# Attention scores scaled by their reciprocal sum on GpSimd in place of ScalarE, in a two-layer encoder on one core

## The chip, the cores and the metric

One Trainium2 chip, one of its cores. The metric is the device time of one execution in microseconds (us). The engines are called by the profile's names: PE is TensorE (PEld its weight loads), DVE is VectorE, ACT is ScalarE, POOL is GpSimd, SP is SyncE, which here issues the DMAs.

## What is computed

Two sequences of 512 tokens, width 1024, go through two layers with shared weights. Layer 0 mixes tokens by dilated window attention (12 heads of 64, in three groups with dilations 1, 4 and 16, ALiBi distances, RMS-normed queries and keys), layer 1 by a gated MLP over chunks; a gated MLP with a width-3 convolution follows each. All is float32. The attention part, cut to what matters here:

```
q = rmsnorm(q.reshape(B, S, N_HEADS_A, HEAD_DIM), g_q)
k = rmsnorm(k.reshape(B, S, N_HEADS_A, HEAD_DIM), g_k)
...
s = s - slopes[:, None, None] * dist
s = jnp.where(valid[:, None], s, NEG_INF)
lse = jax.nn.logsumexp(s, axis=-1)
p = jnp.exp(s - lse[..., None])
o = jnp.einsum('brnihm,brnmhd->brnihd', p, vw)
...
alpha = softmax(stack(lses, axis=0), axis=0)
o = concatenate([outs[g] * alpha[g][..., None] for g in range(N_GROUPS_A)], axis=2)
```

The softmax within a group times the softmax over the three groups is one softmax over the keys of all three groups. So the kernel puts the scores of three heads side by side, 768 columns in all, takes one maximum, one exponential and one sum over them, and multiplies the exponentials by one reciprocal.

## The kernel before

Every matrix product runs on PE; its inputs are split into a high and a low part (`..h` and `..l`, float32r) so that three cheaper products give float32 precision. The order of the work on each engine is written out by hand, and semaphores join the engines.

The change lies in the attention stage of layer 0. It has `NUNIT` = 32 units (2 sequences, 4 head triples `j`, 4 residues `rho`). A unit `n` is a tile of 128 queries by 768 keys (`KEYS`), and passes through these steps:

- PE `scores(n)` (L699 and L701): the three products of queries with keys, into banks 0 and 1.
- DVE `unit(n)`: L1578 adds the distances, in three pieces, into a buffer z; L1585 takes the maximum over its 768 columns and L1587 scales it to the bias of the exponential.
- ACT L1101: the exponential, in place in z, with the row sum in `smax[:, n % 3, 2:3]`.
- DVE `norm(n)` (L1562): the reciprocal of the sum, into `smax[:, n % 3, 3:4]`. It stands in `unit(n + 1)`, behind L1578 and ahead of L1585 there.
- ACT `normed(n)` (L1087): z times that reciprocal, in place. It raises the semaphore `z_done`.
- PE `turn(n)` (L712): waits for `z_done` and transposes the six 128-column blocks of z.
- ACT L1095 copies them from PSUM to `pT`; PE `values(n)` (L731 and L737) multiplies them with the values.
- After each fourth unit, ACT L1123 and L1124 copy the high parts of the outputs and DVE L1451 (`act1l<-bank,act1h`) subtracts them for the low parts.

There are three z buffers: `z[0]`, `z[1]` and the place of `rstd` (the rows write z for the first two and rstd for the third; units 0 and 1 use `z_first`). PE goes through iterations n: `scores(n)`, `turn(n - 2)`, `values(n - 3)`. ACT goes through: L1095 of unit n - 2, `normed(n - 1)`, the exponential of unit n, then what else is due.

The first units share the engines with the end of the step before, the norms of queries and keys: for each of 24 half tiles, ACT squares (L1059, or L1108 for the last two) and copies the high part (L1061, or L1110 for the last two), POOL subtracts it for the low part `sq_low` (L1998, a loop over all 24), PE sums both over the head's rows (L582 and L583), ACT takes the root (L1071) and DVE the reciprocal (L1527, or in halves at L1609). The last two half tiles come in ACT's iterations 0 and 2 of the units. On PE the sum of the last one stands ahead of `values(0)`. ACT needs another table for the root than for the exponential, so a table load stands at each change between them. POOL has nothing to do between its 24th subtraction and the squares of the step after attention.

Of the kernel before, what the change touches and what calls it, by code (L numbers as in the profile page):

```python
# [26 lines left out]
ACT = mybir.ActivationFunctionType  # L27
ALU = mybir.AluOpType
# [7 lines left out]
NS = 2  # L36
# [8 lines left out]
QK_TILES = 2 * KO  # L45
# [5 lines left out]
NUNIT = NS * 4 * R  # L51
# [58 lines left out]
def build(nc, xT, w_qkv, w_o, w_in, w_out, w_up, w_down, wsT, bs, vec, dist, squares, yT):  # L110
    with ExitStack() as ctx:
# [23 lines left out]
        smax, at = place("score_max", [P, 3, 4], F32, at)  # L135
# [52 lines left out]
        for layer, u_at, d_at in ((0, act2_at, act1_at), (1, act1_at, act2_at)):  # L188
            n = f"{layer}"
# [133 lines left out]
        z_rec = sem("z_rec")  # L323
        z_done = sem("z_done")
# [35 lines left out]
        def z_buf(n):  # L360
            if n < 2:
                return z_first[n][:]
            return z_sb[:, n % 3] if n % 3 < 2 else z2_sb
# [606 lines left out]
        def _(act):  # L970
            A = nc.scalar.activation
# [35 lines left out]
            for k, sl in V_ORDER:  # L1007
# [10 lines left out]
              scale=1.0 / D, bias=eps[:, 0:1]).then_inc(v_root, 1)  # L1018
# [61 lines left out]
            for r in range(2):  # L1080
                qk_step(QK_TILES * NS - 4, r, False, True)

            def normed(n):

                act.wait_ge(z_rec, n + 1)
                z = z_buf(n)
                A(z, z, ACT.Copy, scale=smax[:, n % 3, 3:4]).then_inc(z_done, 1)  # L1087

            for n in range(NUNIT + 3):
                u = n - 2  # L1090
                if 0 <= u < NUNIT:
                    act.wait_ge(t_mm, u + 1)
                    if u >= 2:
                        act.wait_ge(pv_mm, u - 1)
                    A(pT[:, u % 2], bank_flat[:, 2 * S:2 * S + KEYS], ACT.Copy).then_inc(t_ev, 1)  # L1095
                if 1 <= n <= NUNIT:
                    normed(n - 1)
                if n < NUNIT:
                    act.wait_ge(z_nmax, n + 1)
                    z = z_buf(n)  # L1100
                    A(z, z, ACT.Exp, scale=HD ** -0.5, bias=smax[:, n % 3, 1:2],  # L1101
                      accum_out=smax[:, n % 3, 2:3]).then_inc(z_exp, 1)
                if n in (0, 2, 4):
                    qk_sqrt(QK_TILES * NS - 3 + n // 2, n // 2 + 1)
                if n in (0, 2):
                    g = n // 2
                    act.wait_ge(up_ev, BANKS + UP_U - 1 + g)
                    A(sq[:], sumsq[:, g], ACT.Square).then_inc(qn_raw, 1)  # L1108
                    act.wait_ge(qn_raw, QK_TILES * NS - 1 + g)
                    A(sq_high[:], sq[:], ACT.Copy).then_inc(qn_high, 1)  # L1110
                if n in (8, 9):

                    if n == 8:
                        act.wait_ge(up_mm, UP_U)
                    ring_hi(WT_WO + n - 8, ows, owh)
                u = n - 3
                if u >= 0 and u % R == R - 1:

                    s, j = u // (4 * R), (u // R) % 4
                    pair = (u // R) % 2  # L1120
                    rows = slice(HD * (j % 2), HD * (j % 2) + HD)
                    act.wait_ge(pv_mm, u + 1)
                    A(act1h[:, j, s], bank[:, 4 + 2 * pair], ACT.Copy).then_inc(o_hi, 1)  # L1123
                    A(act1h[rows, 4 + j // 2, s], bank[rows, 5 + 2 * pair], ACT.Copy).then_inc(o_hi, 1)  # L1124
# [291 lines left out]
            for t in range(KD):  # L1416
                for s in range(NS):
                    n = u_group(t) + s
# [561 lines left out]
        def _(pool):  # L1980
            G = nc.gpsimd
# [11 lines left out]
                    for s in range(NS):  # L1993
                        add(m * NS + (n0 + s), 1, s, sq[:])

            with pool.Fori(0, QK_TILES * NS) as n:
                pool.wait_ge(qn_high, n + 1)
                G.tensor_tensor(sq_low[:], sq[:], sq_high[:].bitcast(F32), ALU.subtract).then_inc(qn_sq, 1)  # L1998
            def ffn(layer):
                mem = ffn_mem[layer]  # L2000
                w0, v0 = layer * NENT, layer * NWIN
# [112 lines left out]
```

## Time and profile before

| | us |
|---|---|
| median of 3 runs | 2043.03 (2042.94 to 2043.03) |
| the profiled execution, its own time | 2045.53 |
| its span, first to last instruction | 2043.7 |
| PE busy | 2008.1, 98% of the span |
| DVE busy | 1245.5, 61% |
| ACT busy | 943.2, 46% |
| POOL busy | 337.0, 16% |
| the attention units, first scores to last values | about 215 to 338 of the span |

All moments below count from the start of the span. The profile's busy shares are means over the whole span; the attention units take up only about 6% of it, so they have to be read on their own, from the timeline and from windows of the stretch. A bracket behind an instruction gives how long its engine sat idle before it, and which instruction ended that.

### The profile page before, as it was taken

To read this page: it belongs to the slowest core of one execution; us is meant where nothing else is said; L and a number is where in the kernel's file an instruction comes from. 1 tells how busy PE (TensorE), PEld (TensorE's weight loads), DVE (VectorE), ACT (ScalarE), POOL (GpSimd) and SP (SyncE) were. 2 spreads that over 40 slices of the span, in tenths; PEclk is the share of its full clock that TensorE was granted. 3 is DMA by queue.
4 is the path that set the end of the run, shared out by engine and by line. 5 is a ranking of instruction groups with operands and counts; after the bars stand their busy time and mean duration, and the time that the engine had idled before them with its cause. 6 is when DMAs were issued, how large, how long until landed. Compare 5 with 4: busy or idle time off the path is not lost.

```text
span 2043.7 us, 24674 instructions
## 1 busy us (share of the span) xinstructions
PE 2008.1 (98%) x9316; PEld 1657.5 (81%) x9316; DVE 1245.5 (61%) x1687; ACT 943.2 (46%) x1445; POOL 337.0 (16%) x238
## 2 busy tenths in 40 slices
PE   8999899998999999999999999999999999999999
PEld 8988567887888888888888888788788888888887
DVE  5288785588776777634536344549877776753433
ACT  6233687645555554423434532334555555542231
POOL 0022100352223223000102000125223223200000
PEclk9999999999999999999999999999999999999999
DMA  5111000412532232444443211141252332244444
GB/s 173 31 42 31 28 17 9 146 52 71 167 93 75 81 93 73 144 142 152 139 165 107 79 41 32 52 144 51 73 175 68 87 93 74 78 160 145 148 140 175
DMA packets 193646, 196.50 MB, mean 96 GB/s; under 512 B 32768, under 2 KB 147968, under 8 KB 193536
## 3 DMA queue, kind: packets, MB, share of 16 engines
q1 hardware_dynamic: 193392, 194.81, 30.7%
q8 instruction: 71, 1.16, 0.2%
q14 instruction: 39, 0.32, 0.1%
q10 hardware_dynamic: 144, 0.21, 0.0%
HBM read 159.33 MB, written 35.65 MB: 95 GB/s over the span
## 4 chain that ended last, share of the span: by engine, by line
PE 82%; issue 12%; DVE 3%; ACT 2%; POOL 0%; POOLq 0%; ACTq 0%; DVEq 0%
PE bank L790 21%; PE bank L791 21%; PE bank L792 21%; PE bank L546 4%; PE bank L547 4%; PE bank L548 4%; PE bank L648 1%; PE bank L649 1%; PE bank L650 1%; PE bank L731 1%; PE bank L712 1%; DVE bl L1451 1%; PE bank L699 1%; PE bank L928 1%; ACT pT L1095 0%
## 5 line engine op out<-in xcount | busy, mean ns | idle before, releaser
L790 PE MATMUL bank<-bh,spl 128*128 128x512 f32 x1064 | 416.2, 391 | 10.7 <-ACT rstd L1200 5.7
L792 PE MATMUL bank<-bh,spl 128*128 128x512 f32 x1064 | 415.2, 390 | 0.0
L791 PE MATMUL bank<-bl,spl 128*128 128x512 f32 x1064 | 415.0, 390 | 0.0
L790 PE MATMUL bank<-hid_h,down_h 128*128 128x512 f32 x704 | 273.9, 389 | 0.0
L791 PE MATMUL bank<-hid_l,down_h 128*128 128x512 f32 x704 | 273.9, 389 | 0.0
L792 PE MATMUL bank<-hid_h,down_l 128*128 128x512 f32 x704 | 273.9, 389 | 0.0
L1451 DVE TENSOR_TENSOR hid_l<-hid_w,hid_h 128x1024 fp32r<-128x1024 f32 x88 | 107.8, 1225 | 269.6 <-ACT hid_h L1334 269.6
L790 PEld LDWEIGHTS bank<-bh,spl 128*128 128x128 f32 x1064 | 200.6, 188 | 55.2 <-ACT rstd L1200 6.6
L792 PEld LDWEIGHTS bank<-bh,spl 128*128 128x128 f32 x1064 | 200.4, 188 | 42.0
L791 PEld LDWEIGHTS bank<-bl,spl 128*128 128x128 f32 x1064 | 200.6, 189 | 41.2
L1334 ACT ACTIVATE hid_h<-hid_w 128x1024 fp32r<-128x1024 f32 x88 | 93.2, 1060 | 297.9 <-DMA down_w<-w_down 297.9
L1451 DVE TENSOR_TENSOR spl<-raw,spl 128x512 fp32r<-128x512 f32 x138 | 107.3, 780 | 130.8 <-ACT spl L1187 130.7
L2015 POOL TENSOR_TENSOR sums<-raw 128x512 f32<-128x512 f32 x76 | 100.0, 1315 | 407.6 <-DVE spl L1451 407.6
L790 PEld LDWEIGHTS bank<-hid_h,down_h 128*128 128x128 f32 x704 | 132.2, 188 | 27.6
L792 PEld LDWEIGHTS bank<-hid_h,down_l 128*128 128x128 f32 x704 | 132.2, 188 | 27.5
L791 PEld LDWEIGHTS bank<-hid_l,down_h 128*128 128x128 f32 x704 | 132.2, 188 | 27.1
L1451 DVE TENSOR_TENSOR spl<-sums,spl 128x512 fp32r<-128x512 f32 x152 | 105.1, 692 | 63.4 <-ACT spl L1187 63.4
L1187 ACT ACTIVATE spl<-sums 128x512 fp32r<-128x512 f32 x152 | 95.6, 629 | 97.8 <-PE bank L792 97.8
L1227 ACT ACTIVATE bank<-gate_out 128x512 f32<-128x512 f32 x88 | 52.7, 598 | 117.7 <-DVE gate_out L1723 117.7
L546 PE MATMUL bank<-act2h,mwh 128*128 128x512 f32 x224 | 88.2, 394 | 1.6 <-DVE act2l L1451 1.5
L1187 ACT ACTIVATE spl<-raw 128x512 fp32r<-128x512 f32 x138 | 85.0, 620 | 8.9 <-DMA raw<-w_up 4.7
L548 PE MATMUL bank<-act2h,mwl 128*128 128x512 f32 x224 | 87.2, 389 | 0.0
(217 smaller groups left out, 3767.5 us busy)
## 6 DMA issues: line engine op xcount, KB each, us to landing
raw<-w_up SPq DMA_DIRECT2D x88, 512.0 KB, 5.4
hid_w<-hidden_kept SPq DMA_DIRECT2D x88, 512.0 KB, 3.4
hidden_kept<-hidden SPq DMA_DIRECT2D x88, 256.0 KB, 2.3
down_w<-w_down SPq DMA_DIRECT2D x88, 256.0 KB, 3.8
x_kept<-x SPq DMA_DIRECT2D x16, 512.0 KB, 6.5
x<-x_kept SPq DMA_DIRECT2D x16, 512.0 KB, 8.7
gws<-w_in SPq DMA_DIRECT2D x32, 256.0 KB, 3.2
qws<-w_qkv SPq DMA_DIRECT2D x24, 256.0 KB, 3.8
```

What stands on the lines that cost most here:

```text
L546: mm(out, wh, ah, start=first, stop=False)
L547: mm(out, wh, al, start=False, stop=False)
L548: return mm(out, wl, ah, start=False, stop=last)
L648: mm(o, xh, gwh[:, sl % 4], start=(k == 0), stop=False)
L790: mm(out, wh, ah, start=first, stop=False, skip_group_check=True)
L791: mm(out, wh, al, start=False, stop=False, skip_group_check=True)
L792: return mm(out, wl, ah, start=False, stop=last, skip_group_check=True)
L1187: A(mem["spl"][n % RING][:, 0], src, ACT.Copy).then_inc(sp_hi, 1)
L1227: A(bank[:, banks(j)[1 + s]], yg[:, s], ACT.Silu).then_inc(silu, 1)
L1334: A(m["hh"][:], m["hw"][:], ACT.Copy).then_inc(d_hi, 1)
L1451: return V.tensor_tensor(out, whole, f(high), ALU.subtract)
L2015: G.tensor_tensor(out, a, b, op).then_inc(w_sum, 1)
```

## The change

The instruction of `normed` leaves ACT. POOL does the same product, in place on the same buffers, with the same semaphores before and behind it. POOL's loop of subtractions ends one earlier, and the last one is written out between the products of units 1 and 2.

```diff
-            def normed(n):
-
-                act.wait_ge(z_rec, n + 1)
-                z = z_buf(n)
-                A(z, z, ACT.Copy, scale=smax[:, n % 3, 3:4]).then_inc(z_done, 1)
-
...
-                if 1 <= n <= NUNIT:
-                    normed(n - 1)
...
-            with pool.Fori(0, QK_TILES * NS) as n:
+            def low_squares(n):
                 pool.wait_ge(qn_high, n + 1)
                 G.tensor_tensor(sq_low[:], sq[:], sq_high[:].bitcast(F32), ALU.subtract).then_inc(qn_sq, 1)
+
+            with pool.Fori(0, QK_TILES * NS - 1) as n:
+                low_squares(n)
+            for n in range(NUNIT):
+                if n == 2:
+                    low_squares(QK_TILES * NS - 1)
+                pool.wait_ge(z_rec, n + 1)
+                z = z_buf(n)
+                G.tensor_scalar(z, z, smax[:, n % 3, 3:4], None, ALU.mult).then_inc(z_done, 1)
```

POOL before, from its loop of subtractions (the loop's body stands once) to the squares of the step after attention:

```order
L1998 TENSOR_TENSOR sq_low<-sq,sq_high 128x512 [waits qn_high]
L1996 REGISTER_ALU
L1996 COMPARE_AND_BRANCH
L1986 COPY sumsq<-sq 128x512 [waits sq_done] x2
L1992 UNCONDITIONAL_BRANCH
```

POOL now, the same place; L1990 is the subtraction, L1999 the product, `score_max` the column with the reciprocal:

```order
L1990 TENSOR_TENSOR sq_low<-sq,sq_high 128x512 [waits qn_high]
L1992 REGISTER_ALU
L1992 COMPARE_AND_BRANCH
L1999 ISA
L1999 TENSOR_SCALAR z_first_84<-z_first_84,score_max 128x768 [waits z_rec]
L1999 TENSOR_SCALAR z_first_85<-z_first_85,score_max 128x768 [waits z_rec]
L1990 TENSOR_TENSOR sq_low<-sq,sq_high 128x512 [waits qn_high]
L1999 TENSOR_SCALAR rstd<-rstd,score_max 128x768 [waits z_rec]
L1999 TENSOR_SCALAR z<-z,score_max 128x768 [waits z_rec] x2
```

One product for each unit now stands on POOL, and the last subtraction stands behind those of units 0 and 1.

ACT before, units 0 to 2 (bank<-bank is the root, pT the copy of the transposed tile):

```order
L1110 ACTIVATE sq_high_73<-sq_62 128x512 [waits qn_raw]
L1087 ACTIVATE z_first0_84<-z_first0_84,score_max_58 128x768 [waits z_rec]
L1101 ACT_TABLE_LOAD
L1101 ACTIVATE z_first1_85,score_max_58<-z_first1_85,score_max_58 128x768 [waits z_nmax]
L1095 ACTIVATE pT_87<-bank 128x768 [waits t_mm]
L1087 ACTIVATE z_first1_85<-z_first1_85,score_max_58 128x768 [waits z_rec]
L1101 ACTIVATE rstd_59,score_max_58<-rstd_59,score_max_58 128x768 [waits z_nmax]
L1071 ACT_TABLE_LOAD
L1071 ACTIVATE bank<-bank,eps_54 128x512 [waits dn_mm]
```

ACT now, the same place; L1102 is the copy of the high part, L1093 the exponential, L1089 the copy to `pT`:

```order
L1102 ACTIVATE sq_high_73<-sq_62 128x512 [waits qn_raw]
L1093 ACT_TABLE_LOAD
L1093 ACTIVATE z_first1_85,score_max_58<-z_first1_85,score_max_58 128x768 [waits z_nmax]
L1089 ACTIVATE pT_87<-bank 128x768 [waits t_mm]
L1093 ACTIVATE rstd_59,score_max_58<-rstd_59,score_max_58 128x768 [waits z_nmax]
L1071 ACT_TABLE_LOAD
L1071 ACTIVATE bank<-bank,eps_54 128x512 [waits dn_mm]
```

The table load and the exponential of unit 1 no longer stand behind the product of unit 0, nor that of unit 2 behind the product of unit 1. The order on PE, DVE and SP is the same.

## Rows read from the trace of the kernel before

**Rows 1.** The page, busy time: us, share of the span, instructions.

```profile
PE 2008.1 (98%) x9316; PEld 1657.5 (81%) x9316; DVE 1245.5 (61%) x1687; ACT 943.2 (46%) x1445; POOL 337.0 (16%) x238
```

**Rows 2.** Windows: length; PE, PEld, DVE, ACT, POOL busy; PE clock; DMA share, GB/s.

```profile
235.00:245.00 10.00, 8.27 (x44) 5.66 (x44) 3.81 (x8) 6.31 (x9) 1.27 (x1) 0.67 0.00 0
245.00:255.00 10.00, 7.37 (x55) 5.08 (x54) 9.86 (x17) 9.91 (x16) 0.00 (x0) 1.00 0.01 2
255.00:265.00 10.00, 9.63 (x68) 6.77 (x69) 8.74 (x22) 7.56 (x12) 0.00 (x0) 0.83 0.01 2
265.00:335.00 70.00, 67.77 (x544) 48.35 (x543) 57.14 (x147) 65.21 (x105) 0.00 (x0) 1.00 0.04 13
```

**Rows 3.** Timeline, one steady unit: start, us, engine, line, operation, tiles, [idle before].

```profile
277.79 0.87 PE L712 MATMUL bank<-ident,z 128*128 128x128 f32 x6
277.93 1.08 DVE L1578 SCALAR_TENSOR_TENSOR rstd<-dist_sb,bank 128x512 f32<-128x512 f32 x3 [0.84 <-PE bank L701]
...
278.93 0.15 DVE L1562 RECIPROCAL score_max<-score_max 128x1 f32<-128x1 f32 x1
...
279.41 0.93 ACT L1087 ACTIVATE z<-z,score_max 128x768 f32<-128x768 f32 x1
...
280.04 0.15 DVE L1587 TENSOR_SCALAR score_max<-score_max 128x1 f32<-128x1 f32 x1
...
280.89 0.88 PE L712 MATMUL bank<-ident,z 128*128 128x128 f32 x6
```

**Rows 4.** Waits from 262 to 336: us in total, times, longest.

```profile
PE bank L712 <- ACT z L1087: 2.0, 4, 1.0
...
PE bank L712 <- ACT rstd L1087: 0.2, 1, 0.2
```

**Rows 5.** Timeline of PE: turns 14, 15 and 30, the last with the longest wait.

```profile
283.79 0.87 PE L712 MATMUL bank<-ident,rstd 128*128 128x128 f32 x6
...
286.66 0.87 PE L712 MATMUL bank<-ident,z 128*128 128x128 f32 x6
...
332.20 0.87 PE L712 MATMUL bank<-ident,z 128*128 128x128 f32 x6 [1.01 <-ACT z L1087]
```

**Rows 6.** Timeline of DVE: the reciprocals of units 15 and 30.

```profile
285.39 0.15 DVE L1562 RECIPROCAL score_max<-score_max 128x1 f32<-128x1 f32 x1
...
330.44 0.15 DVE L1562 RECIPROCAL score_max<-score_max 128x1 f32<-128x1 f32 x1
```

**Rows 7.** Timeline of units 0 to 3, all engines.

```profile
227.35 0.15 DVE L1587 TENSOR_SCALAR score_max<-score_max 128x1 f32<-128x1 f32 x1
...
228.68 0.93 ACT L1101 ACTIVATE z_first<-z_first,score_max 128x768 f32<-128x768 f32 x1
...
229.74 0.16 DVE L1562 RECIPROCAL score_max<-score_max 128x1 f32<-128x1 f32 x1 [0.43 <-ACT z_first L1101]
...
230.79 0.15 DVE L1587 TENSOR_SCALAR score_max<-score_max 128x1 f32<-128x1 f32 x1
...
231.13 0.93 ACT L1101 ACTIVATE rstd<-rstd,score_max 128x768 f32<-128x768 f32 x1
...
235.41 1.27 POOL L1998 TENSOR_TENSOR sq_low<-sq,sq_high 128x512 fp32r<-128x512 f32 x1 [11.67 <-ACT sq_high L1110]
...
236.73 0.79 PE L582 MATMUL bank<-sq_high,heads_r 128*128 128x512 f32 x1 [4.57 <-POOL sq_low L1998]
```

**Rows 8.** Timeline of POOL after attention: one input, two inputs, two inputs and 2048 columns.

```profile
345.01 0.61 POOL L1986 COPY sumsq<-sq 128x512 f32<-128x512 f32 x1 [108.34 <-ACT sq L1160]
...
354.32 1.29 POOL L1989 TENSOR_TENSOR sumsq<-sumsq,sq 128x512 f32<-128x512 f32 x1 [4.57 <-ACT sq L1160]
...
438.57 4.62 POOL L2026 TENSOR_TENSOR x<-x 128x2048 f32<-128x2048 f32 x1 [4.73 <-DVE bl L1451]
```

**Rows 9.** Timeline of DVE beside that last POOL instruction.

```profile
440.57 0.69 DVE L1729 TENSOR_TENSOR hidden<-bank,hidden 128x512 f32<-128x512 f32 x1
441.18 2.55 DVE L1451 TENSOR_TENSOR spl<-raw,spl 128x512 fp32r<-128x512 f32 x1
```

## The prediction, made before the changed kernel was run

> **What bounds the kernel now.** I read the page's busy table first: PE is busy 98% of the span [rows 1], so only what makes PE wait, or run at its lower clock, can move the end. ACT, from which the work is taken, is busy 46%; but that is a mean over the whole span, and the change touches about 6% of it. So the second view is that of windows over the attention units. From 265 to 335 us ACT is busy 65.2 of 70 us, PE 67.8, DVE 57.1 and POOL not at all [rows 2]. ACT is nearly full there, but so is PE, and PE decides.
>
> The third view is the timeline of one steady unit [rows 3]. Two turns of PE (L712) stand at 277.79 and 280.89, 3.10 us apart; the same pair of rows with the other half of the heads gives 283.79 and 286.66, 2.87 us [rows 5]. In both, nothing stands in PE's brackets: PE goes from scores to turn without a wait. The product on ACT runs from 279.41 to 280.34 and is done 0.55 us before the turn starts. So in most units the product is hidden behind PE, and its removal from ACT gives nothing.
>
> The fourth view is the table of waits over the same stretch: PE's turns waited for ACT's product 2.0 us in four cases and 0.2 us in one, the longest 1.0 [rows 4]. These five are the places where ACT first has the high parts of the outputs or of the weights to copy and is late. That is the whole of what a faster ACT can free from 262 us on. Ahead of it two other things bound. Around 236 us PE waits 4.57 us for POOL's last subtraction, which waits for ACT [rows 7]. From 245 to 255 us DVE is busy 9.86 of 10 us [rows 2]: it has the long reciprocals of the last norms between the units, its order is untouched, and a faster ACT does not shorten it.
>
> **What the product costs on POOL.** The trace has no one-input product on POOL, so I bound it. Two inputs: 1.29 us for 512 columns and 4.62 for 2048, that is 2.17 ns a column above 0.18 us [rows 8]; for 768 columns this gives 0.18 + 1.67 = 1.85 us, the upper bound. One input, the copy: 0.61 us for 512 columns, 0.84 ns a column above the same 0.18; 0.83 us for 768, the lower bound. The product reads one tensor, so it is nearest to the copy; I add 0.07 for the reading of the scale column and take **0.90 us**. The Trainium skill (GPSIMD Engine Reference, section Elementwise — side-by-side cycle accounting) has two paces for one input, 1.03 cycles an element for a body of at most two operations and 1.8 for a usual tight loop, which at its 1.2 GHz would be estimates of 0.66 and 1.15 us of pure work; the copy's row agrees with the first, no row here shows the second, and with the second the time would be that of the middle case below.
>
> **Steady units.** The product may start when the reciprocal has ended. I give 0.10 us for that handover and 0.05 for the one to PE (POOL ends at 235.41 + 1.27 = 236.68, PE starts at 236.73 [rows 7]). In the unit of [rows 3] the reciprocal ends at 279.08; with 0.90 the turn could start at 280.13, and PE gets there at 280.89. The tightest ordinary place is a unit behind the low halves on DVE: the reciprocal of unit 15 ends at 285.54 [rows 6], z is ready at 286.59, the turn started at 286.66 [rows 5]. So there is room everywhere, by 0.07 us at the least; of such units in the 2.87 us period there are four. The new late party is nobody: PE itself is next.
>
> Gain from 262 on: the waits other than the longest, 2.0 + 0.2 - 1.0 = 1.2 us, go altogether. At turn 30 PE was free at 332.20 - 1.01 = 331.19 [rows 5]; the reciprocal ends at 330.59 [rows 6], so the turn starts at 330.59 + 0.10 + 0.90 + 0.05 = 331.64 and not at 332.20: 0.56 us. Sum 1.8 us.
>
> **First units.** In units 0 to 2 the product stood ahead of a table load and an exponential. The exponential of unit 1 started at 228.68, while its bias was there at 227.50 [rows 7]; with the product of unit 0 gone and the table loaded beforehand it starts about 1.1 us earlier. DVE's reciprocal of unit 1 waited 0.43 us for it [rows 7]; without that wait the bias of unit 2, which ended at 230.94, ends at 230.51, and the exponential of unit 2, which started at 231.13, starts at 230.56, 0.57 us earlier. Behind it in ACT's order come a table load, the root, the square and the high part, for which POOL's last subtraction waits, for which PE waits: 0.57 us off the 4.57 us wait. POOL's products of units 0 and 1 stand ahead of that subtraction, but are done by about 230.5, five us before it is asked for. The product of unit 1 finishes earlier than on ACT too, which frees PE from a wait before turn 1, but only into the wait for the subtraction. Moving the last subtraction out of the loop costs nothing I can see: the same instruction waits for the same semaphore. The DVE-bound stretch then starts 0.57 us earlier and passes it on; its turns need z later than POOL has it, since a unit takes 4 us there.
>
> **Sum.** 1.8 + 0.57 = 2.3 us, rounded down. Nothing behind attention waits for a fixed time: SP's next loads wait for the last scores to be read and move along with them, and PE is the bound again. Against the profiled execution (2045.53 us, span 2043.7) that is 2043.2; the runs have a median of 2043.03, and I take the difference off that: **2040.7 us**.
>
> **The rivals.**
>
> *POOL in the middle (1.1 to 1.5 us).* The four tight places then cost (D - 0.97) each for a duration D, and the gain at turn 30 shrinks. With 1.34: -1.2 - 0.12 - 0.57 + 4 × 0.37 = -0.4 us, 2042.6. The break-even is near 1.4. For it speaks that this is a different instruction from the copy; against it the copy's pace. The outcome is 2041.5 to 2044.
>
> *POOL as slow as with two inputs, slower than before (1.85 us).* The turn can start 0.14 + 1.00 + 0.15 + 0.10 + 1.85 + 0.05 = 3.29 us after the scores of the next unit end [rows 3], and PE has 3.10 or 2.87 us of work between. The lateness, 0.19 or 0.42, spreads over two units, since one unit of scores always lies between: 0.15 us a unit on average, 24 units, 3.7 us. The tight places: 286.66 becomes 285.54 + 2.00 = 287.54, 0.46 more than the 0.42 already counted, four times, 1.8. Less 0.57 at the start: +4.9 us, **2048**. It decides from a duration of about 1.45 us on. Against it: the product has one tensor input.
>
> *POOL and DVE lock each other out, slower than before.* In [rows 9] DVE's subtraction of two SBUF tensors started at 441.18 and lasted 2.55 us, until just after POOL's instruction ended (438.57 + 4.62 = 443.19); the one before it, with one input in a PSUM bank, took its 0.69 us beside the same POOL instruction. In a unit, L1578 has one bank input and L1585 one tensor; what could be caught is L1587, which scales the maximum. It starts at 280.04, 0.96 us after the reciprocal's end [rows 3], and POOL would be done 0.10 + 0.90 = 1.00 after it: 0.04 us of overlap, no matter. With 1.85 us it is caught 0.99 us in each of 23 units from 265 to 335, 22.8 us; DVE has 70 - 57.1 = 12.9 us free there [rows 2], so the stretch grows by 9.9, less 0.57: **2052.4**. The Trainium skill (SBUF — State Buffer, section Who interferes with whom) gives this rule: DVE and GpSimd share a port pair that the first to issue holds for its whole instruction, and a `tensor_scalar` on DVE is among those that can want it. The trace agrees for the two-tensor subtraction; no row shows it for a one-column `tensor_scalar`. By this rule alone a short product stays harmless and a long one costs twice as much as without it.
>
> *The clock.* PE's granted clock is 0.67 from 235 to 245 and 0.83 from 255 to 265 [rows 2]: between the levels 2.4 and 1.2 GHz, that is 6.6 and 3.4 us at the lower one, both behind PE's waits. With a slightly shorter or shifted wait one of these stretches may go or grow. The second, where PE is the bound, would give back half of 3.4, 1.7 us: 2039.0, or with the first one shortened as well some 2037.5; one more such stretch would cost as much, 2042.4 to 2044. I leave both as they are in the forecast, since the long wait stays 4 us or more.
>
> **How the numbers follow.** Forecast (POOL up to 1.1 us), 2039.5 to 2041.7: 0.52. Middle case: 0.22. Slow without the lock: 0.09. Slow with it: 0.08. Clock otherwise: 0.09, half to each side. The range 2038.5 to 2046.0 holds the forecast, the middle case and two thirds of the clock's; it leaves out about 0.2. A measurement of this kernel can tell about 0.2% from no change, 4.1 us: below 2038.9 is faster, above 2047.1 slower. The forecast of 2.3 us is within it. Faster: part of the clock's case and of surprises, 0.06. Slower: the two slow cases, 0.17. Same: 0.77.
>
> **What would show it.** POOL's product (L1999) should last 0.83 to 1.0 us; above 1.4 the sign is wrong. The waits of PE's turns for z after 262 us should fall from 2.2 to under 0.5 us; the row of turn 30 should have 0.4 to 0.5 in its bracket. PE's wait for the last subtraction should shrink by no more than 0.2 us by its bracket, since turn 1 ends earlier too, but the subtraction should start near 234.8. ACT's busy time falls by about 30 us (32 × 0.93) while the end hardly moves; ACT's gaps before L1089 and L1093 take its place. L1587 should still last 0.15 us; if it lasts 0.5 or more, the lock is there. If the time falls by more than 4 us, the clock rows must show it.

## The result, and the profile after

| | before | after |
|---|---|---|
| median | 2043.03 us | 2050.06 us |
| lowest and highest run | 2042.6 to 2045.16 | 2047.8 to 2050.88 |
| profiled execution, its own time | 2045.53 | 2050.07 |
| its span | 2043.7 | 2048.3 |

The changed kernel takes 1.003 times the time of the kernel before (95% interval 1.0019 to 1.004), 7.0 us more by the medians. The forecast was 2040.7 us, the range 2038.5 to 2046.0: the time lies above the range, on the other side. By the two spans the loss is only 4.6 us; why the two differences disagree is in the experiment on the kernel before.

In the changed kernel POOL's product is L1999 and its last subtraction L1990; ACT's copy to `pT` is L1089 and the exponential L1093; DVE's reciprocal is L1554, the distances L1570, the maximum L1577, its scaling L1579 and the low parts L1443. PE keeps its lines.

First the page's busy times; [rows 1] is the same row of before:

```profile
PE 2007.9 (98%) x9316; PEld 1657.0 (81%) x9316; DVE 1244.6 (61%) x1687; ACT 919.7 (45%) x1413; POOL 407.6 (20%) x270
```

ACT lost its 32 instructions and 23.5 us, and the time rose: ACT was not what the end waited for. POOL gained 70.6 us with 32 instructions, 2.2 us each. The groups of POOL's instructions say the same (busy us, mean ns of one, then the idle time before them):

```profile
L1999 POOL TENSOR_SCALAR z<-z,score_max 128x768 f32<-128x768 f32 x20 | 44.1, 2203 | 27.2 <-DVE score_max L1554 27.2
```

**The product lasts 2.20 us. The upper bound of the prediction was 1.85.** That row alone takes away the forecast's ground (the prediction named 1.4 us as the point from which the sign is wrong); the rest shows what follows from it. The windows, which answer [rows 2] (length; PE, PEld, DVE, ACT, POOL busy; PE clock; DMA share, GB/s):

```profile
235.00:245.00 10.00, 9.30 (x54) 6.46 (x55) 4.41 (x8) 4.82 (x7) 4.54 (x3) 0.75 0.00 0
245.00:255.00 10.00, 7.47 (x62) 5.32 (x62) 9.90 (x21) 7.45 (x12) 4.57 (x3) 1.00 0.01 2
255.00:265.00 10.00, 8.21 (x69) 5.56 (x69) 8.75 (x22) 6.65 (x11) 6.73 (x4) 1.00 0.03 10
265.00:335.00 70.00, 64.34 (x508) 44.83 (x506) 53.98 (x138) 44.78 (x76) 46.55 (x22) 1.00 0.04 11
```

From 265 to 335 us PE is busy 64.34 of 70 us, before 67.77. ACT fell from 65.21 to 44.78, DVE has 16 us free, POOL 23. No engine is full there. This is the mark of a chain of dependences: each engine waits for another in turn. The chain is read in the timeline of one steady unit (start, us, [idle before]), against [rows 3]:

```profile
276.88 0.88 PE L712 MATMUL bank<-ident,z 128*128 128x128 f32 x6
276.99 1.08 DVE L1570 SCALAR_TENSOR_TENSOR rstd<-dist_sb,bank 128x512 f32<-128x512 f32 x3 [1.36 <-PE bank L701]
...
277.99 0.15 DVE L1554 RECIPROCAL score_max<-score_max 128x1 f32<-128x1 f32 x1
...
278.24 2.21 POOL L1999 TENSOR_SCALAR z<-z,score_max 128x768 f32<-128x768 f32 x1 [1.41 <-DVE score_max L1554]
...
279.09 0.15 DVE L1579 TENSOR_SCALAR score_max<-score_max 128x1 f32<-128x1 f32 x1
...
280.49 0.87 PE L712 MATMUL bank<-ident,z 128*128 128x128 f32 x6 [0.45 <-POOL z L1999]
```

The reciprocal ends at 278.14, POOL starts 0.10 later and ends at 280.45, PE's turn starts 0.04 later, after 0.45 us of idling. Both handovers are as forecast. The scores of the next unit ended at 276.92 (L699, 276.33 + 0.59), so the path from scores to turn is 3.57 us; the prediction's sum, 0.14 + 1.00 + 0.15 + 0.10 + D + 0.05, gives 3.64 for D = 2.20. The 0.07 between them are in the first term: L1570 starts 0.07 after the scores' end, and the 0.14 were counted from the start of the turn, which is a little earlier. The waits from 262 to 345, for [rows 4]:

```profile
PE bank L712 <- POOL z L1999: 4.9, 11, 1.2
PE bank L712 <- POOL rstd L1999: 2.2, 6, 0.5
```

7.1 us in 17 turns stand where 2.2 us in five stood. At the start the products of units 0 and 1 now end late too, yet the last subtraction comes earlier; these rows of PE and POOL answer [rows 7]:

```profile
226.52 0.50 PE L582 MATMUL bank<-sq_high,heads_r 128*128 128x512 f32 x1
...
230.82 0.87 PE L712 MATMUL bank<-ident,z_first 128*128 128x128 f32 x6 [1.04 <-POOL z_first L1999]
...
233.90 1.26 POOL L1990 TENSOR_TENSOR sq_low<-sq,sq_high 128x512 fp32r<-128x512 f32 x1 [3.13 <-ACT sq_high L1102]
...
235.21 0.79 PE L582 MATMUL bank<-sq_high,heads_r 128*128 128x512 f32 x1 [3.52 <-POOL sq_low L1990]
```

Between the two L582 rows lie 8.69 us. Before, the earlier L582 stood at 227.44 and the later at 236.73, 9.29 apart: 0.60 us are gained, 0.57 were forecast. PE's wait shrank by more than the forecast 0.2, from 4.57 to 3.52: besides the 0.60, turn 1 ran 0.46 us later (4.30 us after the earlier L582, and 3.84 before), since it waited 1.04 us for POOL. The prediction had it run earlier. Behind that, from 244 to 258 us, four turns wait for POOL:

```profile
244.03 0.87 PE L712 MATMUL bank<-ident,z 128*128 128x128 f32 x6 [0.49 <-POOL z L1999]
...
248.65 0.88 PE L712 MATMUL bank<-ident,z 128*128 128x128 f32 x6 [1.25 <-POOL z L1999]
...
252.47 0.87 PE L712 MATMUL bank<-ident,rstd 128*128 128x128 f32 x6 [0.66 <-POOL rstd L1999]
...
257.10 0.87 PE L712 MATMUL bank<-ident,z 128*128 128x128 f32 x6 [1.16 <-POOL z L1999]
```

### The profile page after: what moved, and what is told of

Read it like the earlier page. It is cut to its first block, busy times and chain, and to the rows that moved or that the text cites. A ratio compares the mean times of both kernels' runs of the same rounds, so it can differ in the third digit from the quotient of the medians.

```text
span 2048.3 us, 24671 instructions
## 1 busy us (share of the span) xinstructions
PE 2007.9 (98%) x9316; PEld 1657.0 (81%) x9316; DVE 1244.6 (61%) x1687; ACT 919.7 (45%) x1413; POOL 407.6 (20%) x270
## 4 chain that ended last, share of the span: by engine, by line
PE 91%; DVE 5%; ACT 1%; POOL 1%; issue 1%; DMA 0%; SPq 0%; ACTq 0%; DVEq 0%
PE bank L790 21%; PE bank L792 21%; PE bank L791 21%; PE bank L546 6%; PE bank L548 6%; PE bank L547 6%; PE bank L648 1%; PE bank L650 1%; PE bank L649 1%; PE bank L606 1%; PE bank L607 1%; PE bank L608 1%; PE bank L731 1%; DVE bl L1443 1%; POOL z L1999 1%
## 5 line engine op out<-in xcount | busy, mean ns | idle before, releaser
L1443 DVE TENSOR_TENSOR hid_l<-hid_w,hid_h 128x1024 fp32r<-128x1024 f32 x88 | 107.8, 1225 | 269.6 <-ACT hid_h L1326 269.6
L1443 DVE TENSOR_TENSOR spl<-raw,spl 128x512 fp32r<-128x512 f32 x138 | 107.3, 780 | 131.2 <-ACT spl L1179 131.1
L1443 DVE TENSOR_TENSOR spl<-sums,spl 128x512 fp32r<-128x512 f32 x152 | 105.1, 692 | 63.2 <-ACT spl L1179 63.2
L547 PE MATMUL bank<-act2l,mwh 128*128 128x512 f32 x224 | 87.2, 389 | 0.0
```

Source lines behind the costliest of these rows:

```text
L547: mm(out, wh, al, start=False, stop=False)
L1443: return V.tensor_tensor(out, whole, f(high), ALU.subtract)
```

## The experiments

**The measure.** The time of a kernel is the median of all its runs, given with the ratio to the runs of before that were made beside it. Single executions of one kernel differ by 2.6 to 6.8 us, as much as what is looked for, so the traces are compared by a stretch of their own: from PE's sum of the second-last half tile (L582, 226.52 above) to the start of its last turn (turn 31). It holds the attention units and neither what precedes nor what follows them. The column "clock" is PE's granted clock from 255 to 260 us. In the changed kernel turns 7, 30 and 31 are:

```profile
260.45 0.87 PE L712 MATMUL bank<-ident,z 128*128 128x128 f32 x6 [0.41 <-POOL z L1999]
...
336.69 0.88 PE L712 MATMUL bank<-ident,z 128*128 128x128 f32 x6 [1.24 <-POOL z L1999]
...
340.01 0.82 PE L712 MATMUL bank<-ident,z 128*128 128x128 f32 x6
```

In the second trace of the kernel before, the start of the stretch and turns 7 and 30:

```profile
226.96 0.50 PE L582 MATMUL bank<-sq_high,heads_r 128*128 128x512 f32 x1
...
260.06 0.88 PE L712 MATMUL bank<-ident,z 128*128 128x128 f32 x6
...
330.93 0.87 PE L712 MATMUL bank<-ident,z 128*128 128x128 f32 x6 [1.01 <-ACT z L1087]
```

Its turn 31 starts at 334.28.

| kernel | product, us | stretch, us | clock | median, us | ratio, 95% interval |
|---|---|---|---|---|---|
| before, first trace | 0.93 on ACT | 108.11 | 0.66 | 2043.03 | |
| before, again | 0.93 on ACT | 107.32 | 1.00 | 2043.19 | 0.9999 [0.9989, 1.0009] |
| copy for the product | 0.83 | 103.75 | 1.00 | 2040.58 | 0.999 [0.9981, 0.9999] |
| two operations, second a constant | 0.90 | 103.98 | 1.00 | 2041.19 | 0.9989 [0.998, 0.9998] |
| two operations, columns | 0.98 | 104.11 | 1.00 | 2038.94 | 0.9982 [0.9973, 0.9991] |
| the same again | 0.98 | 104.15 | 1.00 | 2039.29 | 0.9986 [0.9977, 0.9995] |
| one operation, half the columns | 1.24 | 107.24 | 0.68 | 2041.69 | 0.9993 [0.9984, 1.0002] |
| broadcast column as second input | 1.47 | 109.33 | 0.67 | 2044.23 | 1.0002 [0.9993, 1.0011] |
| changed kernel | 2.20 | 113.49 | 1.00 | 2050.06 | 1.003 [1.0019, 1.004] |
| the same again | 2.20 | 113.92 | 1.00 | 2049.87 | 1.0027 [1.0016, 1.0038] |
| on POOL for units 0 and 1 only | 2.20 | 106.55 | 1.00 | 2044.54 | 1.0003 [0.9994, 1.0012] |
| on POOL from unit 2 on only | 2.20 | 113.83 | 1.00 | 2049.25 | 1.003 [1.0018, 1.0042] |

**Theory.** The instruction's length alone makes the loss; the place on POOL, the handovers and the new order are harmless. Rivals: POOL's product is long because something beside it holds it up; the form or the place costs PE or DVE something whatever the length; the loss comes from the first units, not the steady ones.

### What the forms cost by themselves

Nine instructions on POOL at the start of the program, each waiting for the one before it, with nothing beside them on POOL; the attention units as in the changed kernel. Its one execution took 2050.76 us. Three of them:

```diff
+            G.tensor_copy(q, q).then_inc(probe, 1)
...
+            G.tensor_scalar(q, q, one, None, ALU.mult).then_inc(probe, 1)
...
+            G.tensor_scalar(q, q, one, one, ALU.mult, ALU.add).then_inc(probe, 1)
```

> The changed kernel with nine GpSimd instructions on the idle tile sq ahead of its first loop, each alone, to price them: a copy of 512 and of 256 columns, the product with a scale column on 512, 256 and 128 columns, with a constant, an addition in place of the product, product and addition in one, and the two-input form with the scale column broadcast. In the trace of the changed kernel the product on 768 columns took 2.203 us. Theory 1, a pace of its own of about 2.6 ns a column above 0.18 us: 512 columns 1.5 us, 256 columns 0.85, 128 columns 0.52; the constant and the addition cost the same. Theory 2, a fixed cost for the scale column (2.20 - 0.83 = 1.37 us above the copy): 512 columns 2.0 us, 256 columns 1.8, and the constant costs 0.61 as a copy does. The broadcast form should cost what two inputs cost, 1.29 us.

The timeline of POOL in the first 15 us (the copy, the product with a column over 512, 256 and 128 columns, the one with two operations, and the broadcast column as second input):

```profile
1.74 0.61 POOL L1999 COPY sq<-sq 128x512 f32<-128x512 f32 x1
...
2.91 1.57 POOL L2003 TENSOR_SCALAR sq<-sq,eps 128x512 f32<-128x512 f32 x1
4.57 0.92 POOL L2005 TENSOR_SCALAR sq<-sq,eps 128x256 f32<-128x256 f32 x1
5.58 0.60 POOL L2007 TENSOR_SCALAR sq<-sq,eps 128x128 f32<-128x128 f32 x1
...
9.71 0.76 POOL L2013 TENSOR_SCALAR sq<-sq,eps 128x512 f32<-128x512 f32 x1
10.56 1.04 POOL L2015 TENSOR_TENSOR sq<-sq,eps 128x512 f32<-128x512 f32 x1
```

From 256 to 512 columns the product with one operation costs 0.65 us, 2.54 ns a column above 0.27; for 768 columns that is 2.22, and 2.20 was measured in the kernel. So it is slow for itself, and nothing beside it holds it up: DVE runs nothing from 2.91 to 4.48 us, while POOL has the 1.57 us of the first product. A constant in place of the column gave 1.67, an addition 1.58: it is the form with one operation. **Two operations take 0.76, half of what one takes.** No row of the trace of before shows an instruction of this kind on POOL.

### The same place, the copy's length

```diff
-                G.tensor_scalar(z, z, smax[:, n % 3, 3:4], None, ALU.mult).then_inc(z_done, 1)
+                G.tensor_copy(z, z).then_inc(z_done, 1)
```

> The changed kernel with a GpSimd copy of z onto itself in place of the product, so the scaling is left out; all waits stay. It should last 0.83 us (0.61 for 512 columns scaled by the pace 0.84 ns). Theory A, the loss comes from the duration of the GpSimd instruction alone, through the path scores, distances, reciprocal, product, turn: then this is the forecast's case, 2.3 us below the kernel before, some 2041, and PE's waits for z after 262 us fall under 0.5 us in all. Theory B, the loss comes from the fourth engine in the path, its handovers or its port, whatever the instruction lasts: then it stays 3 us or more above the kernel before.

The copy leaves out the scaling; the waits and their order are those of the changed kernel. 2040.58 us; the forecast, made for a product of 0.90 us, was 2040.7. That the two agree to 0.1 us is in part luck: the stretch is 3.6 us shorter than that of before with full clock, where 2.3 were forecast. The wait left after 262 us:

```profile
PE bank L712 <- POOL z L1999: 0.3, 1, 0.3
```

The copies in the groups of POOL:

```profile
L1999 POOL COPY z<-z 128x768 f32<-128x768 f32 x20 | 16.6, 829 | 49.1 <-DVE score_max L1554 49.1
```

Same engine, same order, same semaphores, and the loss is gone. The length is what matters, and place and order are harmless.

### A length between

```diff
-                G.tensor_scalar(z, z, smax[:, n % 3, 3:4], None, ALU.mult).then_inc(z_done, 1)
+                G.tensor_tensor(z, z, smax[:, n % 3, 3:4].to_broadcast([P, KEYS]), ALU.mult).then_inc(z_done, 1)
```

> The changed kernel with the product as a two-input GpSimd instruction, the scale column broadcast over the 768 columns; nothing left out. By the rows of two inputs it should last 1.85 us and not 2.20. Theory A: 0.35 us less in the path, of which half shows in each of about 24 units, 4.2 us less than the changed kernel, and so 2 to 3 us above the kernel before. Theory B: the time of the changed kernel.

I had expected the pace of two full tensors, 1.85 us; a column that is repeated is cheaper, 1.47. The time, 2044.23, is 1.5 us over that of before beside it (2042.76), but the interval of the ratio includes 1. The stretch tells more: 109.33 against 108.11 for before, both with the lowered clock from 255 to 260.

### The first two units alone, and all but these

In the one kernel POOL has the products of units 0 and 1, with the last subtraction behind them, and ACT has the others. In the other kernel ACT has these two and POOL the rest, behind its last subtraction. POOL's products raise a semaphore of their own in both, for which PE's turns wait. The two edits in ACT's loop:

```diff
-                if 1 <= n <= NUNIT:
+                if 3 <= n <= NUNIT:
```

> Only units 0 and 1 are multiplied on GpSimd, with the last subtraction behind them; units 2 to 31 stay on ScalarE. Semaphores of its own for the two. Theory A: the exponentials of units 1 and 2 start earlier and the last subtraction with them, by 0.57 us, and nothing else changes: 0.6 us below the kernel before, with the five waits for ScalarE from 262 us on as they were (2.2 us). If the clock's low stretch near 256 us goes as it did in the changed kernel, up to 1.7 us more. Theory B has a fourth engine in only two units: no change from before.

```diff
-                if 1 <= n <= NUNIT:
+                if 1 <= n <= 2:
```

> The other side of the run of units 0 and 1: these two stay on ScalarE, GpSimd multiplies units 2 to 31 with the one-operation form of 2.20 us, the last subtraction is ahead of them. Theory A: the gain of 0.57 us in the first units is gone, the loss of the steady units stays; 0.6 us or more above the changed kernel, and 6 to 8 us above the kernel before. If instead the loss came from the first units, where a 2.20 us product delays turns 0 and 1, the time would be near the kernel before.

With the first two alone the stretch is 0.77 us shorter than that of before with full clock (106.55 and 107.32), and from turn 6 to turn 31 the two take 77.44 and 77.49 us: all of it is in the first units. In the time it can't be seen; the median is 2044.54 against 2042.76, and the runs stand in two clusters, 2041.5 to 2042.8 and 2044.5 to 2044.9, of which the profiled one (2042.84) belongs to the lower. With the others alone the sums of the norms lie 9.28 us apart again, as in before, and the stretch is 6.5 us longer. So the gain of 0.6 us sits in units 0 and 1, and the loss in the units behind them. Its waits after 262 us are those of the changed kernel: 4.9 us in 11 turns and 2.2 us in 6. It was expected 0.6 us or more above the changed kernel, and that did not come: its stretch lies between the two of the changed kernel (113.49 and 113.92), and its median, 2049.25, is below theirs.

### The kernel before, once more

> The kernel before, unchanged, for a second trace. Its first trace had PE's clock at the lower level twice in the attention units, from 235 to 242 and from 255 to 259 us, and ran 2045.53 us where the median is 2043.0; the trace of the changed kernel has the first stretch only. Theory C: the second stretch comes and goes from run to run of the same kernel, and costs the 2.3 us between the two times. Then a run of this kernel near 2043 has a granted clock of 1.00 from 255 to 260, and one near 2045 has 0.66 there. If a run near 2043 has the second stretch too, the 2.3 us lie elsewhere.

The window from 255 to 260 us of the kernel before, in its first trace (columns as above):

```profile
255.00:260.00 5.00, 4.63 (x28) 3.35 (x30) 4.42 (x12) 2.56 (x5) 0.00 (x0) 0.66 0.00 0
```

The same window in its second trace:

```profile
255.00:260.00 5.00, 4.68 (x42) 3.10 (x38) 4.93 (x14) 3.59 (x5) 0.00 (x0) 1.00 0.00 0
```

The same kernel had 0.66 in one execution, so a third of the time at full speed and the rest at 1.2 GHz, and 1.00 in the other. Turn 6 starts 31.55 us after L582 in the first and 29.83 in the second; at turn 31 0.8 us of these 1.7 are left. The first profiled execution took 2045.53 us where the median is 2043.03, the second 2042.80. Of the 2.7 us between the spans 0.8 are this stretch's, 0.5 lie ahead of it (L582 at 227.44 and 226.96) and 1.4 behind it, none of them in what the change touches. Against the second, the changed kernel's span is 7.3 us longer and its stretch 6.2 us.

### A faster form of the same product

The theory above, that the length alone decides (theory A in the expectations), says that the change is good with a short product. Two operations are short; the second multiplies by a column of ones, so that the result is the same number. (POOL also waits once, at the start, until that column is loaded.)

```diff
-                G.tensor_scalar(z, z, smax[:, n % 3, 3:4], None, ALU.mult).then_inc(z_done, 1)
+                G.tensor_scalar(z, z, smax[:, n % 3, 3:4], ones[:, 0:1], ALU.mult, ALU.mult).then_inc(z_done, 1)
```

> The changed kernel with the same product written as a GpSimd tensor_scalar of two operations, times the reciprocal column and then times a column of ones; nothing left out, the result bit for bit that of one product. In the price run this form with two operations took 0.76 us for 512 columns, against 1.57 with one operation. For 768 columns that is 1.0 to 1.1 us. Theory A (time follows the instruction's duration): at the four tight places the turn is late by under 0.15 us each, the rest is the forecast: 1.5 to 2.2 us below the kernel before, some 2041. If the two-operation form owed its price to something else in that run (its place behind others), it lasts 2.2 us and the time is the changed kernel's, 7 us above.

**2038.94 us**, 0.9982 of before (0.9973 to 0.9991). The lead is larger than the 1.5 to 2.2 us expected: 4.5 by the medians, 3.2 by the stretches. What lies outside the stretch was not explained. The product in the groups of POOL:

```profile
L2000 POOL TENSOR_SCALAR z<-z,score_max,ones 128x768 f32<-128x768 f32 x20 | 19.6, 981 | 46.2 <-DVE score_max L1554 46.2
```

PE's turn 30, which answers the last of [rows 5]:

```profile
326.74 0.87 PE L712 MATMUL bank<-ident,z 128*128 128x128 f32 x6 [0.54 <-POOL z L2000]
```

It is the only wait for POOL after 262 us. In the window from 265 to 335 PE is busy 69.45 of 70 us:

```profile
265.00:335.00 70.00, 69.45 (x555) 50.20 (x554) 54.23 (x141) 46.26 (x79) 21.58 (x22) 1.00 0.02 7
```

### Which two operations

Seven more forms at the start of the program, as in the first probe; the attention units as in the changed kernel. Its one execution took 2048.15 us.

```diff
+            G.tensor_scalar(q, q, one, one, ALU.mult, ALU.mult).then_inc(probe, 1)
...
+            G.tensor_scalar(q, q, one, 1.0, ALU.mult, ALU.mult).then_inc(probe, 1)
...
+            G.tensor_scalar(q, q, 2.0, 1.0, ALU.mult, ALU.mult).then_inc(probe, 1)
```

> Seven more prices on GpSimd, as in the first price run, each alone on the idle tile: the product of two operations (times a column, times a column) on 512 and 256 columns, with a column and a constant, with two constants, times a column plus a column, the broadcast form on 256 columns, and last the product of one operation on 512 columns again. If the one-operation form is slow for itself: 0.76, about 0.5, 0.76, 0.76, 0.76, 0.6 and 1.57 us. If the order of the instructions made the difference in the first run, the last one is fast or the first one slow.

The timeline of POOL (two columns over 512 and 256 columns; column and constant; two constants):

```profile
1.79 0.77 POOL L1999 TENSOR_SCALAR sq<-sq,eps 128x512 f32<-128x512 f32 x1
2.66 0.55 POOL L2001 TENSOR_SCALAR sq<-sq,eps 128x256 f32<-128x256 f32 x1
3.31 0.69 POOL L2003 TENSOR_SCALAR sq<-sq,eps 128x512 f32<-128x512 f32 x1
4.08 0.62 POOL L2005 TENSOR_SCALAR sq<-sq 128x512 f32<-128x512 f32 x1
```

All forms with two operations are fast, 0.86 ns a column, the pace of the copy; each scale that is a column costs some 0.07 us more. The form with one operation, in the last place here (6.54 to 8.42 us), took 1.88 us where it had 1.57 in the other probe. What ran beside it differs: here DVE had L1461, with two inputs in SBUF, beside it for 1.55 us, and there DVE was idle. In the first probe the form with a constant had L1461 beside it for 1.34 us and took 1.67. That L1461 lengthens it is likely and was not tested; so the 0.10 of the constant may come from there too.

### One chip, four versions

The last four ran in the same rounds on one chip.

```diff
-                G.tensor_scalar(z, z, smax[:, n % 3, 3:4], None, ALU.mult).then_inc(z_done, 1)
+                G.tensor_scalar(z[:, 0:KEYS // 2], z[:, 0:KEYS // 2], smax[:, n % 3, 3:4], None, ALU.mult) \
+                    .then_inc(z_done, 1)
```

> The product in its one-operation form on GpSimd, but over 384 of the 768 columns only; the other half of the weights stays unscaled, so this part of the computation is left out. By the rows of the nine forms (0.27 us and 2.53 ns a column) it should last 1.24 us. Theory A (the length of the instruction decides, break-even near 1.4 us): PE's turns wait for it 1 to 2.5 us in all from 262 us on, against 2.2 us for the kernel before, and the 0.6 us of the start are gained: turn 31 0.5 to 1 us after what it is with the copy, the time 2041.5 to 2042.8. Theory B (the form itself costs PE something, whatever its length): the loss of the changed kernel stays at half or more, 2046 or above.

```diff
-                G.tensor_scalar(z, z, smax[:, n % 3, 3:4], None, ALU.mult).then_inc(z_done, 1)
+                G.tensor_scalar(z, z, smax[:, n % 3, 3:4], 1.0, ALU.mult, ALU.mult).then_inc(z_done, 1)
```

> The changed kernel, with the product as two operations, the second a multiplication with the constant 1.0. From the 512-column rows of the second probe (two columns 0.77, column and constant 0.69, two constants 0.62) and the 0.98 us of the product with two columns I expect 0.85 to 0.92 us. Theory A: the time is that of the version with two columns, 2038 to 2041, since both are under the 1.0 us that stay hidden. Theory B (the fast pace needs two columns): 2.2 us and 2050.

> The product with two operations, both scales columns of SBUF, once more, on the same chip and in the same rounds as the changed kernel and the kernel before. Theory A: 0.98 us a product, 2 to 4 us under the kernel before and some 10 us under the changed kernel. If its earlier lead came from the clock of that chip alone, it is within 1 us of the kernel before.

> The changed kernel itself, for comparison on one chip: 2.20 us a product, 2049 to 2051, 6 to 7 us over the kernel before. Nothing else is expected by any theory; it gives the difference that the other three of this set are to be held against.

Half the columns (the scaling of the other half is left out) took 1244 ns and 2041.69 us; PE waited 1.5 us after 262 us (1.0 and 0.5). The form with one operation does no harm when it is short, so the rival on the form falls. The stretch is 107.24 us, 0.87 below that of before with the same lowered clock, and with 1.47 us it is 1.22 above it: the line between the two crosses zero at 1.24 + 0.23 × 0.87 / 2.09 = **1.34 us**. The prediction had put the break-even near 1.4. The line joins two forms by one trace each, and in the one of 1.47 us two of DVE's subtractions are longer by 0.39 us each (last section), so the second digit is not sure. Turn 31 was expected 0.5 to 1 us after that of the copy; it comes 3.5 us after it by the stretch, of which 2.3 lie ahead of turn 6, where the lowered clock is, and 1.2 behind it.

The version with a constant took 904 ns, within the 0.85 to 0.92 us expected, and 2041.19 us, 0.2 above the 2038 to 2041 expected; the one with two columns took 2039.29, 10.6 us under the changed kernel (2049.87) and 3.8 under the kernel before (2043.12). Between 0.83 and 0.98 us the stretches differ by 0.4 us at most and rise with the length, while the medians do not follow this order. That the slightly longer product has the lower median is therefore not its doing; the single runs of these versions spread over 2038.1 to 2043.9. What can be said is that the copy and the two forms with two operations are faster than before, by 1.9 to 4.5 us by the medians and 2.0 to 3.7 by the ratios; the intervals of the copy and of the constant end just below 1, at 0.9999 and 0.9998.

## Why the prediction was wrong, point by point

**The step that failed is the price of the product.** The text bounded it by the copy (0.83) and by the two-input pace (1.85) and took 0.90, with "the product reads one tensor, so it is nearest to the copy". It lasted 2.20. The number of inputs was the wrong measure: the slow one has one input and one operation, the fast one has one input and two. The upper bound rested on the belief that one input can't cost more than two, and no row showed that. The Trainium skill (GPSIMD Engine Reference, section Elementwise — side-by-side cycle accounting), weighed in the prediction, gives 1.03 cycles an element for a body of at most two operations; at the 1.2 GHz given there that is an estimate of 0.86 ns. The copy and the products with two operations agree with it (0.84 and 0.86 ns a column); the product with one operation, 2.54 ns or 3.0 cycles, does not. The section's other pace, 1.8 cycles, is its best case of a tight loop, not the usual one as the prediction had it, so it could not serve as an upper bound either.

**The slow rival had the right mechanism and a length that was too short.** Its path from scores to turn, 1.44 us + D, gives 3.64 us at 2.20. PE's own work between is 3.10 or 2.87 [rows 3, 5]. The lateness, 0.54 or 0.77, spreads over two units: 2.985 + 0.66 / 2 = 3.31 us a unit. Measured, from turn 7 at 260.45 to turn 30 at 336.69: 76.24 / 23 = 3.315. Over the 25 units from turn 6 to turn 31 the kernel took 82.91 us, and before 77.49 with full clock. The text's last term, the tight places behind the low halves, does not stand beside that one: with a unit of 3.3 us DVE is ahead of PE there again. PE's turns around such a place:

```profile
283.62 0.87 PE L712 MATMUL bank<-ident,rstd 128*128 128x128 f32 x6 [0.18 <-POOL rstd L1999]
...
287.02 0.88 PE L712 MATMUL bank<-ident,z 128*128 128x128 f32 x6 [0.45 <-POOL z L1999]
...
290.15 0.87 PE L712 MATMUL bank<-ident,z 128*128 128x128 f32 x6 [0.18 <-POOL z L1999]
```

The steps are 3.40 and 3.13, as elsewhere; the text would have added 0.46 us in each of four such places. Whether they count at 1.85 us was not measured. The text also set its 24 units against units without waits. The kernel before has its own there: from turn 7 to turn 30 it took 70.87 us in the second trace (260.06 to 330.93), 3.08 a unit. So the loss is 0.23 us a unit and not 0.33, 5.4 us in 23.

**"Its turns need z later than POOL has it"**, for the stretch bound by DVE, was true for 0.9 us only. With 2.20 us four turns from 244 to 258 waited 0.49 to 1.25 us, and of the 0.60 us gained at the norms nothing is left by turn 7: it starts 33.93 us after L582, and before 33.10. From there to turn 31 the loss is 79.56 - 74.22 = 5.34 us, and 0.83 + 5.34 = 6.2 us is what the stretch lost.

**What held.** The gain at the start, 0.57 us, was measured as 0.60 (9.29 to 8.69). With a product of 0.98 us the turns from 7 to 31 take 71.79 us where the second trace of before took 74.22, 2.4 us less; the forecast for it was 1.8, from the waits of the first trace, and the second trace had one wait more, of 0.49 us. The wait of turn 30 was to be 0.4 to 0.5 us with a product of 0.90, and is 0.54 with one of 0.98. ACT's busy time was to fall by 30 us and fell by 23.5, since the products had overlapped their neighbours on ACT: in the unit of [rows 3] the copy before the product ended at 279.51, 0.10 us after the product's start, and the exponential started at 280.24, 0.10 before its end.

**The lock.** The rival said that DVE's scaling of the maximum would wait for a long product on POOL. In the unit shown, L1579 ran at 279.09, inside POOL's product (278.24 to 280.45), and took 0.15 us as before; over the 23 of them from 262 to 345 the mean is 153 ns. By this rule the time would have been 2052.4 at 1.85 us, and more at 2.20. It was not the lock.

**The sum against the profiled execution.** It was made against 2045.53 and then moved to the median by taking off the difference. That was right. But the first profiled execution was 2.5 us longer than the median, and so the two spans of the result show 4.6 us of loss where the second trace of before shows 7.3, near the 7.0 of the medians.

**The odds.** The two slow cases together had 0.17, which rested on the nearness of the product to the copy. The price of the one instruction that the whole change adds was open by more than a factor of two, the break-even lay inside the bounds, and so it should have had more.

## What to carry to other kernels

Before an instruction moves to another engine, measure its very form there (operation count, scale column, width): input count does not rank forms on POOL, and a needless second operation made this product more than twice as fast (0.98 us for 2.20). Then work out the break-even from the timeline first, as the room between the last input's end and the consumer's start; that part of this prediction (1.4 us, and 1.34 by the line between two forms) held, and it says at once how exact the price has to be. When an engine is 98% busy over the span, look in the stretch that the change touches for the point at which the path between engines becomes longer than the work on that engine.

## What the runs showed of the hardware

**One operation costs more than two on GpSimd.** `tensor_scalar` on float32 with one operation takes 2.5 ns a column (1.57 us for 512, 2.20 for 768); with two it takes 0.86 (0.77 for 512, 0.98 for 768). A broadcast column as the second input of `tensor_tensor` costs 1.04 us for 512 columns, two full tensors 1.29 [rows 8].

**A two-tensor instruction of DVE beside a product on GpSimd.** In the changed kernel DVE's subtraction of the output weights ran within POOL's product (timeline of POOL and DVE):

```profile
261.36 2.20 POOL L1999 TENSOR_SCALAR rstd<-rstd,score_max 128x768 f32<-128x768 f32 x1 [0.96 <-DVE score_max L1554]
...
262.29 0.95 DVE L1443 TENSOR_TENSOR owl<-ows,owh 128x768 fp32r<-128x768 f32 x1
```

In the first trace of the kernel before, with nothing on POOL, the same subtraction took as long:

```profile
264.18 0.95 DVE L1451 TENSOR_TENSOR owl<-ows,owh 128x768 fp32r<-128x768 f32 x1
```

The product and the subtraction in the version with the broadcast column:

```profile
262.51 1.47 POOL L1999 TENSOR_TENSOR rstd<-rstd,score_max 128x768 f32<-128x768 f32 x1 [1.41 <-DVE score_max L1554]
...
263.45 1.34 DVE L1443 TENSOR_TENSOR owl<-ows,owh 128x768 fp32r<-128x768 f32 x1
```

Beside the one-operation product it takes 0.95 us, wholly inside POOL's 261.36 to 263.56. Beside the two-input form, with which it overlaps for 0.53 us (263.45 to 263.98), it takes 1.34, so 0.39 more. The Trainium skill (SBUF — State Buffer, section Who interferes with whom) has a DVE instruction with two SBUF inputs contend with any GpSimd instruction that reads SBUF. The pair with the broadcast column and [rows 9] agree; the pair with the product does not, since that GpSimd instruction read SBUF too and DVE was not held up. The two probes show the same difference on a subtraction over 384 columns (DVE L1445): 0.56 us within a product with one operation (4.92 us, first probe), 0.97 where a product with two operations and then the broadcast form ran beside it (5.00 us, second probe). Which of these two held it up was not separated.

**The lowered clock comes and goes.** PE's clock is at 1.2 GHz for a stretch behind its wait of 3.5 to 4.8 us near 235 us in every trace (0.50 granted from 235 to 237). Its length varies too: from 241 to 245 us the changed kernel had 1.00 in its first trace and 0.50 in its second, whose turn 7 comes 0.43 us later after L582; that is the whole difference of their stretches. A second such stretch, from 255 to 260 us, stood in one trace of the kernel before and was absent from the other, and stood in two of the other versions; where it stood in before it cost 1.7 us at once, of which 0.8 were left at turn 31. Its cause was not settled.
